# Eight more weight blocks by seven quarter products, and half as many parts of plain blocks between the steps of attention

## The reference

```python
h = x @ w_in[i]
ua, va, za, qh, kh, vh, zb, ga, gb = jnp.split(h, IN_OFFSETS, axis=-1)   # nine results, 1024 columns each
...
ya = ua * sa.reshape(bn, s_len, A_WIDTH) * jax.nn.silu(za)
q = apply_rope(qh...) * (B_QK_DIM ** -0.5)
k = apply_rope(kh...)
...
sc = jnp.einsum("bqhmd,bkhmd->bhmqk", qblk, k)          # 8 heads, 2 maps each, 8 blocks of 128 queries, causal
pr = jax.nn.softmax(sc, axis=-1)
a = pr[:, :, 0] - lam * pr[:, :, 1]
o = jnp.einsum("bhqk,bkhd->bqhd", a, v)
...
o = rms_norm_2(o, b_subln_g[i]) * (1.0 - lam_init)
yb = o.reshape(bn, s_len, B_WIDTH) * jax.nn.silu(zb)
merged = jax.nn.sigmoid(ga) * (ya @ w_branch_a[i]) + jax.nn.sigmoid(gb) * (yb @ w_branch_b[i])
ple = jax.nn.sigmoid(x @ w_ple_gate[i]) * (p[i] @ w_ple[i])
```

## Time and profile before

| | |
|---|---|
| time, median of 3 runs | 2334.25 us (2333.76 to 2336.13) |
| the profiled execution: its own time, its span | 2335.22 us, 2333.1 us |
| TensorE busy | 2300.7 us, 99% of the span |
| DVE, ACT, POOL busy | 1260.1 (54%), 965.1 (41%), 773.9 (33%) us |
| quarter blocks run | from 1072 to 1341 us of the span |
| attention's eight heads run | from 1396 to 2022 us of the span |

### The profile page before, as it was taken

How to read it: one execution, slowest core, us unless ns; L and a number is a source line. 1 busy time by engine, 2 the same in 40 slices (tenths; PEclk the granted TensorE clock), 3 DMA queues, 4 the chain that set the end, 5 groups by cost and what they waited for, 6 DMA issues and landing times.

```text
span 2333.1 us, 37390 instructions
## 1 busy us (share of the span) xinstructions
PE 2300.7 (99%) x14608; PEld 1994.1 (85%) x14608; DVE 1260.1 (54%) x2509; ACT 965.1 (41%) x1891; POOL 773.9 (33%) x773
## 2 busy tenths in 40 slices
PE   8999999999999999999999999999999999999998
PEld 7889978899888999887888889988998887788887
DVE  4013359999998323471333255445444545478756
ACT  5125665555554442332223223444444444555320
POOL 3121324534543221414444333324332332232113
PEclk9999999999999999999999999999999999999999
DMA  6234344443334521232333253432343244384631
GB/s 251 99 117 171 120 146 149 134 155 113 126 128 161 191 100 64 99 118 96 111 116 113 101 158 130 132 118 84 116 137 113 86 137 164 129 286 173 228 109 72
DMA packets 137159, 312.13 MB, mean 134 GB/s; under 512 B 12320, under 2 KB 51872, under 8 KB 125728
## 3 DMA queue, kind: packets, MB, share of 16 engines
q1 hardware_dynamic: 80352, 223.85, 28.3%
q10 hardware_dynamic: 56640, 86.00, 9.9%
HBM read 211.77 MB, written 98.04 MB: 133 GB/s over the span
## 4 chain that ended last, share of the span: by engine, by line
PE 93%; DVE 3%; ACT 1%; DMA 1%; issue 1%; POOL 0%; ACTq 0%; DVEq 0%; SPq 0%; POOLq 0%
PE bank L416 12%; PE bank L418 12%; PE bank L417 12%; PE bank L427 6%; PE bank L428 6%; PE bank L429 6%; PE bank L2048 4%; PE bank L2049 4%; PE bank L2050 4%; PE bank L2755 3%; PE bank L2732 3%; PE bank L507 3%; PE bank L509 3%; PE bank L508 3%; PE bank L1623 2%; PE bank L2721 1%
## 5 line engine op out<-in xcount | busy, mean ns | idle before, releaser
L416 PE MATMUL bank<-at_hi,w_hi 128*128 128x512 f32 x1280 | 522.4, 408 | 2.8 <-DVE at_lo L2390 1.0
L418 PE MATMUL bank<-at_hi,w_lo 128*128 128x512 f32 x1280 | 500.5, 391 | 0.0
L417 PE MATMUL bank<-at_lo,w_hi 128*128 128x512 f32 x1280 | 499.3, 390 | 0.0
L427 PE MATMUL bank<-w_hi,at_hi 128*128 128x256 f32 x1152 | 338.7, 294 | 0.5 <-issue 0.5
L429 PE MATMUL bank<-w_hi,at_lo 128*128 128x256 f32 x1152 | 326.3, 283 | 0.0
L428 PE MATMUL bank<-w_lo,at_hi 128*128 128x256 f32 x1152 | 326.2, 283 | 0.0
L382 POOL TENSOR_TENSOR w_lo<-w_raw,w_hi 128x2048 fp32r<-128x2048 f32 x41 | 190.4, 4644 | 402.1 <-ACT w_hi L395 375.7
L304 POOL TENSOR_TENSOR small<-small,cols 128x1 f32<-128x1 f32 (+1 forms) x162 | 47.7, 294 | 743.9 <-ACT da_junk L2668 393.2
L416 PEld LDWEIGHTS bank<-at_hi,w_hi 128*128 128x128 f32 x1280 | 241.2, 188 | 56.1 <-issue 7.3
L418 PEld LDWEIGHTS bank<-at_hi,w_lo 128*128 128x128 f32 x1280 | 240.2, 188 | 52.5
L417 PEld LDWEIGHTS bank<-at_lo,w_hi 128*128 128x128 f32 x1280 | 241.1, 188 | 43.7
(11 more groups left out here) (343 smaller groups left out, 4649.2 us busy)
## 6 DMA issues: line engine op xcount, KB each, us to landing
w_raw<-in_weights SPq DMA_DIRECT2D x84, 1024.0 KB, 5.9
feat<-stage ACTq DMA_DIRECT2D x184, 256.0 KB, 2.0
tok<-stage ACTq DMA_DIRECT2D x72, 256.0 KB, 2.2
stage<-feat SPq DMA_DIRECT2D x32, 256.0 KB, 3.7
w_mem<-in_w_mem SPq DMA_DIRECT2D x4, 1024.0 KB, 6.8
x<-in_x SPq DMA_DIRECT2D x4, 1024.0 KB, 11.3
logg<-gate_g ACTq DMA_DIRECT2D x8, 512.0 KB, 2.9
rec_b<-logg SPq DMA_DIRECT2D x16, 256.0 KB, 5.0
```

Source lines behind the costliest of these rows:

```text
L416: nc.tensor.matmul(ps_gemm[i % 2], wh, ah, start=(k == 0), stop=False)
L417: nc.tensor.matmul(ps_gemm[i % 2], wh, al, start=False, stop=False)
L418: last = nc.tensor.matmul(ps_gemm[i % 2], wl, ah, start=False, stop=(k == KT - 1))
L427: nc.tensor.matmul(o, ah, wh, start=(k == 0), stop=False)
```

## The change

Two segments of four blocks each (`ZA`, and the first half of what was a segment of eight, `GA`) go from the list beside attention to the list of quarter blocks: 22 quarter blocks, and 12 plain blocks beside attention (`VA` in form T, `PG` in form T, then the last four in form F). In the table of slots, each slot before a turn and each slot before an output holds 1 part in place of 2; in the last head's block 7 it is 2 and 1 in place of 3 and 2. First, between and last slots stay. The weights are laid out in DRAM in the new order, and one wait for stores of SP names the segment that is left.

```diff
@@ gemm_quarters
             Segment(4, "F", ACT.Copy, feat2, QF),
             Segment(4, "F", ACT.Copy, feat2, KF),
             Segment(4, "F", ACT.Silu, feat2, ZB),
+            Segment(4, "F", ACT.Copy, feat2, ZA),
+            Segment(4, "F", ACT.Copy, feat2, GA),
             Segment(2, "F", ACT.Copy, feat2, UA),
@@
-        SLOT_PARTS = [[2] + [2, 0, 2] * LONG + [2, 1, 2] * LONG + [1]] * (B_HEADS - 1) + [
-            [4] + [2, 0, 2] * LONG + [2, 1, 2] * (LONG - 1) + [3, 1, 2] + [3]]
+        SLOT_PARTS = [[2] + [1, 0, 1] * LONG + [1, 1, 1] * LONG + [1]] * (B_HEADS - 1) + [
+            [4] + [1, 0, 1] * LONG + [1, 1, 1] * (LONG - 1) + [2, 1, 1] + [3]]
         SLOT_PARTS[0] = [5] + SLOT_PARTS[0][1:]
@@ gemm_att
             Segment(4, "T", ACT.Copy, tok2, VA),
-            Segment(4, "F", ACT.Copy, feat2, ZA),
             Segment(4, "T", ACT.Copy, tok2, PG),
-            Segment(8, "F", ACT.Copy, feat2, GA),
+            Segment(4, "F", ACT.Copy, feat2, GA + 4 * CB),
@@ p8_sp
-            all_stored(sp, gemm_att[:2])
+            all_stored(sp, gemm_att[:1])
```

More of the change, by code:

```diff
@@ L3453 @@
     gate_p = a["w_ple_gate_2"][0]
-    quartered = quarters(np.concatenate([w2[:, 3072:5120], w2[:, 6144:7168], w2[:, 0:512]], 1))
+    quartered = quarters(np.concatenate([w2[:, 3072:5120], w2[:, 6144:7168], w2[:, 2048:3072], w2[:, 7168:8192], w2[:, 0:512]], 1))
     weights = np.concatenate([quartered if w is None else blocks(w) for w in (
@@ L3462 @@
         w2[:, 512:1024],
-        w2[:, 1024:2048], w2[:, 2048:3072], gate_p, w2[:, 7168:],
+        w2[:, 1024:2048], gate_p, w2[:, 8192:],
         a["w_branch_b_2"][0], a["w_branch_a_2"][0], a["w_out_2"][0])], 0)
```

## The result

The changed kernel takes **2353.1 us** (median of four, 2350.9 to 2354.7), the kernel before 2334.2 (four, 2333.8 to 2336.1). The ratio is 1.0077, 95% interval 1.0063 to 1.0091: slower by 19 us, where 8.9 were forecast. That is outside the forecast's own 2339 to 2349 us and at the very end of the wider range of 2332 to 2353. The profiled execution took 2354.71 us with a span of 2352.9, that of before 2335.22 and 2333.1. Two single executions further down, one of the kernel before (2832.9 us) and one of the 20 and 14 blocks (3221.8 us), ran at a mean clock of 0.75 and 0.66 and are left out of the ratios.

What follows compares the result with a forecast made beforehand. The prediction took TensorE's streamed columns to bound the kernel. Its terms, -21.8 + 7.7 + 3.3 + 3.0 + 7.7 + 7.3 + 1.7 = +8.9 us on 2334.25, gave 2343 us; own range 2339 to 2349, wider 2332 to 2353.

Steps and rivals of the forecast that it cites:

- eight blocks: Eight plain blocks leave attention (174.1 us) and return as quarter blocks at 19.04 us each (152.3 us): -21.8 us.
- end of head: Next head's first scores wait for the keys' low part, seven times, longer in heads 0, 4 and 6: +7.7 us.
- turn of block 7: Turn waits for DVE's rows, slack 2.6 us against two parts removed, seven times, more in heads 1 and 5: +3.3 us.
- scores of blocks 4 to 7: Scores wait for the previous block's exponentials where ACT has an evacuation ahead of the copy, seven times: +3.0 us.
- POOL's low parts: Low parts queued ahead of the next root delay the norm, in heads 1, 3, 4 and 6: +7.7 us, from 3 to 11.
- head 7: In the last head, the mask, Gelu and a table load delay turns of blocks 3, 4 and block 6's scores: +7.3 us.
- clock: Idle TensorE drops to 1.2 GHz; one slow stretch counted, at head 7's two long waits: +1.7 us, ends 0 and 14.
- One sign of being wrong: In attention, new waits ahead of L2742 beyond the only one expected, in head 4, would show the forecast wrong.
- the step on the mask: Head 7: the mixing weights' mask, 4.98 us on DVE, delays block 3's rows; slack 1.20 against three parts, 2.9 us lost.
- no change: Rival: waits cancel the gain, POOL's delay mostly absorbed and the clock holds; +2.5 us, 2337 us, chance 0.27.
- faster: Rival: chains follow TensorE, freeing head 7 and POOL's place, no slow clock; -4.8 us, 2329.5 us, chance 0.12.
- much slower: Rival: attention turns latency-bound, jitter costs 7 us and slow stretches in each head 5; +21, 2355 us, chance 0.15.

Runs made afterwards that it cites:

- 20 and 14 blocks: Changed kernel with 20 quarter blocks and 14 beside attention, POOL's low parts one slice at a time, slot parts moved, head 7's statistics later: 2330.1 us.
- filled waits: Changed kernel with extra products, 15.7 us of streaming, in the ten longest waits of attention, none cured: 2343.0 us.
- full slots: Changed kernel with matmuls issued twice in slots before turns and outputs (head 7's two-part slot: one part only), keeping each slot's old columns: 2490.7 us.
- version of 2324.8 us: Changed kernel, low parts one slice at a time, eight parts moved from first slots to later ones, head 7's statistics one query block later: 2324.8 us.

## Why the prediction was right in direction and short in size

In the sum of the prediction, by terms (us; what was measured is the change's profiled execution against before's):

| term | forecast | measured |
|---|---|---|
| eight blocks | -21.8 | -21.8 |
| end of head | +7.7 | +8.9 |
| turn of block 7 | +3.3 | +1.7 |
| scores of blocks 4 to 7 | +3.0 | +1.9 |
| POOL's low parts | +7.7 | +11.0 |
| head 7 | +7.3 | +4.0 (3.1 over before's 0.9) |
| clock | +1.7 | +13.6 (10 by the filled waits) |

**Blocks.** Right. ACT's splits in two neighbouring quarter blocks of after (to the earlier trace rows) are again 19.04 us apart, and full slots gave the same from the other side:

```profile
1095.99 1.91 ACT L2140 ACTIVATE w_hi<-w_raw 128x2048 fp32r<-128x2048 f32 x1
...
1115.03 1.91 ACT L2140 ACTIVATE w_hi<-w_raw 128x2048 fp32r<-128x2048 f32 x1
```

**Waits.** 27.6 us against 29.0, inside the 26 to 32 that were to show the forecast right; the places are nearly all those named. One sign of being wrong came up, though: waits ahead of L2742 (now L2743) were expected in head 4 alone, and they stand in heads 1, 3, 4 and 6, 3.0 us in sum. There the late root delays the transpose of the normed output itself, and not the scores alone; it is part of the POOL term. So the prediction's way to the waits, place by place from slack, held, though its errors partly cancelled. (The single waits are read from the trace; the table of waits above sums the same ones by line.)

*End of head*: right, seven waits. Five are 0.70 to 1.23 us. The two of over 2 us are heads 4 and 6, which the prediction did mark as having low parts beside the splits, but at 1.2 and 0.6 us more than the others, and not 1.5 and 1.8. Timelines of DVE and PE, after, ends of heads 4 and 5 (to the earlier trace rows):

```profile
1843.43 2.25 DVE L2429 SCALAR_TENSOR_TENSOR da_q_lo<-da_q,da_q_hi 128x1024 fp32r<-128x1024 f32 x1 [3.67 <-ACT da_q_hi L2424]
...
1846.87 0.47 PE L2756 MATMUL bank<-da_k_hi,da_q_hi 64*128 64x128 f32 x2 [2.25 <-DVE da_k_lo L2431]
...
1906.22 1.23 DVE L2429 SCALAR_TENSOR_TENSOR da_q_lo<-da_q,da_q_hi 128x1024 fp32r<-128x1024 f32 x1 [3.30 <-ACT da_q_hi L2424]
...
1908.64 0.33 PE L2756 MATMUL bank<-da_k_hi,da_q_hi 64*128 64x128 f32 x2 [0.74 <-DVE da_k_lo L2431]
```

DVE's split takes 2.25 us beside POOL's low parts (1839.57 to 1844.59) and 1.23 without.

*POOL*: the mechanism was right, and removing it gave the largest single gain. Heads 3 (2.9 for 2.9), 4 (1.4 for 1.2) and 6 (2.1 for 2.3) came as walked through; head 1 lost 2.8 and not 1.3; and in head 5 block 3's end cost 1.7 us, where "ends in block 3 and later find heads long enough" allowed nothing. That sentence was wrong.

*Head 7*: the step on the mask failed. It read the mask's 4.98 us as the instructions' own length and let it stand in the way of block 3's turn. After:

```profile
1992.96 1.70 DVE L2914 TENSOR_TENSOR sm_ws<-sm_ws,lst 128x128 f32<-128x128 f32 x8
...
1995.34 0.75 DVE L2536 SCALAR_TENSOR_TENSOR da_a<-da_p,small 128x512 f32<-128x512 f32 x1
...
2001.87 2.68 DVE L2931 BATCH_NORM_STATS2 small<-sm_v 128x6 f32<-128x512 f32 x4 [3.32 <-ACT sm_v L2816]
...
2006.15 0.66 PE L2722 MATMUL bank<-ident,da_a 128*128 128x128 f32 x4 [3.74 <-DVE da_a L2536]
```

The mask took 1.70 us. Before, POOL's low parts (5.26 us from 1960.91) had run beside 4.0 of its 4.98 us; the new table has them elsewhere. So the turn of block 3 had 0.5 us to spare. The other half, the turn of block 4 behind Gelu, came as forecast: 3.7 us. The sum of the term was off too: its own numbers, 2.9 + 2.7 - 0.6 + 1.0, give 6.0 us and not 7.3, since before's 0.9 is no new loss.

**Clock.** This is the step that failed and made the forecast short: "The slow stretch behind the first runs into the second, so I count one: +1.7". It counted only the waits of 3 and 4 us of head 7, though its one example, stood at a wait of 2.3 us, and put one stretch a head (14 us) at the far end. That end was then left out of the forecast's own range: with it the range would have reached 2355 us and more, and not 2349. The change has five stretches for 30.6 us, four at waits of 1.8 to 2.6 us, which the prediction had forecast itself (POOL's and the ends of heads, at 1.3 to 2.9 us) but not priced for clock. Filling the waits without curing them gave back 10.1 us, 8.4 more than the 1.7 of the forecast. By the stretches' length it is 11.9 more, and with waits 1.4 us below the forecast this about makes up the gap between forecast (8.9) and measurement (19.0). The Trainium skill, TensorE: Matmul & The Clock Gate, Part 1, was weighed in the prediction with 1.7 us for each long wait. That idleness puts the clock back, the traces bear out; that half of the slow time is lost, they do not quite (10 us for 27.2, below). The error was in what counts as long.

The rivals: no change and faster are out. The last one, much slower (2355), comes nearest in size, for its slow stretches in most heads (it gave them 5 us); jitter was not seen, as two profiles of the changed kernel have nearly the same waits.

## What to carry to other kernels

When work that fills waits is taken from beside a chain, price each new wait twice, for itself and for the slow clock behind it; here waits of some 2 us did that, and the second price was a third to a half of the first (10.1 and 13.6 us against 28.1). Before giving up such a change, look at what is queued in whole lumps ahead of a small instruction of the chain (here 6 us of low parts ahead of a root of 0.2 us), and cut the lumps up: that turned 19 us lost into some 3 gained, and placing the parts by the slack of each slot into nearly 12. A duration read where two engines overlapped is not the instruction's; and a table of counts that sets where tiles end is worth trying at a shift of one.

## What the runs showed of the hardware

- Waits of 1.7 to 2.6 us are enough for a slow stretch of 3.4 or 6.8 us, but not each time: four of the seven in attention in the change's profile had one, and of the same waits, the one of 2.2 us ahead of head 5 had 6.8 us behind it in one profile and none in two others. The wait of 2.3 us ahead of head 0 stands alike in twelve of the fourteen profiles: one has 6.8 us at it, six 3.4 and five none.
- A slow stretch cost less than half its length: 27.2 us of it cost some 10 (waits filled), and the two profiles of the changed kernel, 6.7 us apart in it, differ by 2.0 us with 0.8 us more idle time in the shorter.
- DVE instructions that read two SBUF operands take longer beside POOL's tensor_tensor: the eight of the mask 4.98 and 1.70 us, the split of the queries 2.25 and 1.23 (in head 6 1.98, and that of the keys 2.28), the rows of 512 columns 2.08 and 0.75. The norm, which reads a PSUM bank, took 0.40 us beside POOL's rotation (1738.08 us in the version of 2324.8 us) and 0.41 at 1959.96 us of before without. The Trainium skill, SBUF — State Buffer, Who interferes with whom, says just this: a DVE instruction with two SBUF inputs contends with a GpSimd instruction that reads SBUF, one with at most one, outside DVE's two-port modes, does not. The traces agree with it.
